# 290 TensorE products in 25 forms placed behind the last stage of a float32 transformer kernel

## What is computed

```python
for i in range(4):                       # first block
    x = x + 0.5 * rms_norm(swiglu_ffn(rms_norm(x, g[0]), w_gate_up[i, 0], w_down[i, 0]), g[1])
    y = mixer_a / mixer_b / mixer_c / mixer_a (rms_norm(x, g[2]), memory of 256 rows, ...)
    x = x + rms_norm(y, g[3])
    x = x + 0.5 * rms_norm(swiglu_ffn(rms_norm(x, g[4]), w_gate_up[i, 1], w_down[i, 1]), g[5])
for i in range(4):                       # second block: nsa, stick breaking, conv, moba
    x = x + mixer_i(_rms_norm(x, attn_norm[i]), ...)
    hm = _rms_norm(x, mlp_norm[i])
    x = x + jnp.square(jax.nn.relu(hm @ mlp_w_up[i])) @ mlp_w_down[i]
return x
```

## Time and profile before

| what | value |
|---|---|
| median of 2 runs | 3338.68 us (3338.37 to 3338.98) |
| span of the profiled execution, first to last instruction | 3335.1 us |
| TensorE matmuls busy | 3215.7 us, 96% of the span, 19661 instructions |
| VectorE busy | 1953.3 us, 59% |
| ScalarE busy | 1628.6 us, 49% |
| mean granted TensorE clock | 0.992 |

### The profile page before, as it was taken

One profiled execution on the slowest core, in us unless ns is written; L12 is line 12 of the kernel. 1 busy time (PEld: TensorE's weight loads), 2 busy tenths in 40 slices (PEclk: granted clock), 3 DMA queues, 4 the chain that ended last, 5 costly groups with the idle time before them and its releaser, 6 DMA issues.

```text
span 3335.1 us, 52167 instructions
## 1 busy us (share of the span) xinstructions
PE 3215.7 (96%) x19661; PEld 2816.0 (84%) x19661; DVE 1953.3 (59%) x2911; ACT 1628.6 (49%) x2426; POOL 135.6 (4%) x230
## 2 busy tenths in 40 slices
PE   7999999999999999999999999999999999999999
PEld 7977988977898977897987897779788888987797
DVE  4566556665555554655656656565566558656663
ACT  5445444445444435544545545554354446545552
POOL 1000000000000000000000101000000000001000
PEclk9999999999999999999999999999999999999999
DMA  6654656652555543565654554435444551555354
GB/s 215 194 174 133 201 177 192 189 157 89 175 185 185 180 157 114 158 190 166 206 192 152 179 190 152 140 112 184 162 158 142 187 179 33 195 189 164 116 200 152
DMA packets 413280, 551.71 MB, mean 165 GB/s; under 512 B 33952, under 2 KB 263520, under 8 KB 413104
## 3 DMA queue, kind: packets, MB, share of 16 engines
q1 hardware_dynamic: 409248, 536.10, 50.1%
q0 software_dynamic: 2864, 10.38, 1.0%
q10 hardware_dynamic: 992, 2.84, 0.2%
HBM read 548.15 MB, written 1.05 MB: 165 GB/s over the span
## 4 chain that ended last, share of the span: by engine, by line
PE 87%; DVE 8%; ACT 3%; issue 1%; POOL 0%; DMA 0%; SPq 0%; DVEq 0%; ACTq 0%
PE G L796 16%; PE G L800 15%; PE G L797 15%; PE G L897 11%; PE G L899 11%; PE G L898 11%; DVE ring_lo_sb L1977 3%; PE T L775 2%; PE S L1000 1%; PE O L1028 1%; DVE act_hi_sb L1991 1%; ACT ring_hi_sb L1438 1%; DVE act_lo_sb L2001 1%; DVE work_sb L2181 0%; PE G L1307 0%
## 5 line engine op out<-in xcount | busy, mean ns | idle before, releaser
L1977 DVE TENSOR_TENSOR ring_lo_sb<-ring_sb,ring_hi_sb 128x1024 fp32r<-128x1024 f32 (+1 forms) x1028 | 1222.4, 1209 | 620.2 <-ACT ring_hi_sb L1438 602.4
L1438 ACT ACTIVATE ring_hi_sb<-ring_sb 128x1024 fp32r<-128x1024 f32 (+1 forms) x1028 | 1056.7, 1044 | 693.3 <-DMA ring_sb<-ffn_w_down 218.3
L897 PE MATMUL G<-act_hi_sb,ring_hi_sb 128*128 128x256 f32 x3136 | 876.4, 279 | 3.0 <-DVE ring_lo_sb L1977 3.0
L898 PE MATMUL G<-act_lo_sb,ring_hi_sb 128*128 128x256 f32 x3136 | 872.3, 278 | 0.0
L899 PE MATMUL G<-act_hi_sb,ring_lo_sb 128*128 128x256 f32 x3136 | 872.3, 278 | 0.0
L897 PEld LDWEIGHTS G<-act_hi_sb,ring_hi_sb 128*128 128x128 f32 x3136 | 589.5, 188 | 3.3 <-issue 3.2
L796 PE MATMUL G<-ring_hi_sb,hid_hi_sb 128*128 128x512 f32 x1456 | 581.0, 399 | 10.3 <-DVE hid_hi_sb L2010 6.5
L899 PEld LDWEIGHTS G<-act_hi_sb,ring_lo_sb 128*128 128x128 f32 x3136 | 589.8, 188 | 0.0
L898 PEld LDWEIGHTS G<-act_lo_sb,ring_hi_sb 128*128 128x128 f32 x3136 | 588.3, 188 | 0.0
L797 PE MATMUL G<-ring_lo_sb,hid_hi_sb 128*128 128x512 f32 x1456 | 576.9, 396 | 0.0
L800 PE MATMUL G<-ring_hi_sb,hid_lo_sb 128*128 128x512 f32 x1248 | 492.5, 395 | 0.0
(11 more groups left out here) (274 smaller groups left out, 2543.1 us busy)
## 6 DMA issues: line engine op xcount, KB each, us to landing
ring_sb<-ffn_w_gate_up SPq DMA_DIRECT2D x704, 256.0 KB, 4.0
ring_sb<-ffn_w_down SPq DMA_DIRECT2D x352, 256.0 KB, 3.8
ring_sb<-mlp_w_up SPq DMA_DIRECT2D x256, 256.0 KB, 3.8
ring_sb<-mlp_w_down SPq DMA_DIRECT2D x256, 256.0 KB, 3.7
ring_sb<-a_w_in SPq DMA_DIRECT2D x48, 256.0 KB, 4.4
ring_sb<-sb_w_in SPq DMA_DIRECT2D x48, 256.0 KB, 4.0
ring_sb<-moba_w_in SPq DMA_DIRECT2D x48, 256.0 KB, 4.0
ring_sb<-w_mem_kv SPq DMA_DIRECT2D x32, 256.0 KB, 3.8
```

What stands on the lines that cost most here:

```text
L897: mm(dst, hi, act_hi[:, kt, :], start=(kt == 0 and f == 0), stop=False, skip_group_check=True)
L898: mm(dst, hi, act_lo[:, kt, :], start=False, stop=False, skip_group_check=True)
L1438: fn(ring_hi[:, s_, :, 0:w], ring[:, s_, :, 0:w], ACT.Copy).then_inc(hi_ready, 1)
L1977: v.tensor_tensor(ring_lo[:, s_, :, 0:w], ring[:, s_, :, 0:w], ring_hi[:, s_, :, 0:w], ALU.subtract).then_inc(lo_ready, 1)
```

## The change

At the end of TensorE's stream, behind the loop over the stages, code is added that issues 25 blocks. A block is 8, 11 or 12 rounded products into the PSUM bank `T[0]` (in one block `T[0]` and `T[1]` in turn) and then one float32 transpose of the constant `from_on` into the same bank, which marks the block's end in a trace. No product waits for a semaphore or raises one, and nothing reads what they write. No other engine's code changes.

```diff
                 elif kind == "conv":
                     conv()
+            def flat(b, at):
+                return b[:, at, :, :].rearrange("p k n -> p (k n)")
+
+            def block_of(n_mm, lhs, rhs, bank=lambda j: 0, first=lambda j: j == 0):
+                for j in range(n_mm):
+                    w, m = lhs(j), rhs(j)
+                    b = T[bank(j)]
+                    dst = b[0:w.shape[1], 0:int(np.prod(m.shape[1:]))]
+                    if len(m.shape) == 3:
+                        dst = dst.rearrange("p (a n) -> p a n", a=m.shape[1])
+                    mm(dst, w, m, start=first(j), stop=True, skip_group_check=True)
+                nc.tensor.transpose(T[0][:, 0:P], from_on, ident)
+
+            def tail_forms():
+                a_flat = act_hi[:, :, :].rearrange("p k n -> p (k n)")
+                h_flat = hid_hi[:, :, :].rearrange("p k n -> p (k n)")
+
+                def acts(off=0, m=P, step=1):
+                    return lambda j: a_flat[:, 2 * P * (j % 6) + off:2 * P * (j % 6) + off + m * step:step]
+
+                def units(off=0, n=HALF, step=1):
+                    return lambda j: flat(ring_hi, j % RING)[:, off:off + n * step:step]
+                block_of(12, acts(), units())
+                block_of(12, acts(m=32), units())
+                block_of(12, acts(), units(off=8))
+                block_of(12, acts(), units(off=16))
+                block_of(12, acts(), units(off=32))
+                block_of(12, acts(off=16), units())
+                block_of(12, acts(off=8), units())
+                block_of(12, acts(step=2), units())
+                block_of(12, acts(), units(step=2))
+                block_of(12, acts(), lambda j: ring_hi[:, j % RING, :, 0:SEQ])
+                block_of(12, acts(), units(n=480))
+                block_of(12, acts(), units(n=448))
+                block_of(12, acts(), units(n=384))
+                block_of(12, acts(), units(n=320))
+                block_of(12, acts(), units(), bank=lambda j: j % 2)
+                block_of(12, acts(), units(), first=lambda j: True)
+                block_of(12, lambda j: flat(ring_hi, j % RING)[:, 0:P], lambda j: h_flat[:, HALF * j:HALF * (j + 1)])
+                block_of(12, lambda j: a_flat[:, 0:P], lambda j: flat(ring_hi, 0)[:, 0:HALF])
+                block_of(8, lambda j: a_flat[:, 0:P], lambda j: flat(ring_hi, 0)[:, 0:64])
+                for n in (264, 272, 282, 300, 320, 340):
+                    block_of(11, acts(), lambda j, n=n: flat(ring_hi, j % RING)[:, 0:n if j == 0 else SEQ])
+            tail_forms()
```

## The result

The changed kernel took 3394.35 us (median of 3387.9 and 3400.8) against 3338.68 us before, a ratio of 1.0169 with an interval of 1.0143 to 1.0195. Forecast were 3397.0 us and +1.7%, within a range of 3390 to 3403. The two executions of the changed kernel lie 12.9 us apart, those of the kernel before 0.6 us. That spread turned out to be the part of the case that I had not foreseen, and most of the experiments are about it.

What follows compares the result with a forecast made beforehand. TensorE, with matmuls busy 96% of the span, was taken as the bound; 62.5 us of added work from 3330.60, behind 4.5 us of cover, lengthens the span 58.3 us, giving 3397.0 us (+1.7%), range 3390 to 3403.

Steps and rivals of the forecast that it cites:

- What bounds the end: End of the span: TensorE done at 3330.60, then idle 4.5 us until the store lands, covering that much added work.
- the sign of being wrong: End of the span: more than 0.5 us after TensorE's last transpose would show the prediction wrong.
- The price by columns: Added products: cost goes by columns, 0.4557 ns each, 0.2333 us for 512; thirteen ordinary blocks 36.4 us.
- the rival of a lost fast path: Added blocks: one shifted or stepped form priced as plain float32, 7.5 us above the ordinary price; chance 0.13.
- The cover of the stepped stationary operand: Block with every second element stationary: a weight load of twice 106 ns stays hidden, ordinary price of 0.2333 us a product.
- The stepped moving operand: Block whose moving operand takes every second element: twice the ordinary price, 5.6 us, between bounds of 2.8 and 10.3 us.
- Narrow products: Block of eight 64-column products: about 0.12 us each, 1.0 us together, limited by the 128-column weight load.
- The array's rate: Rival for the 168 wide products: all at 0.2133 us, 3.4 us less, and the step free, 2.8 us less; chance 0.09.
- The clock: Added work: granted clock stays 1.0; the half clock would add 0.19 us a wide product, sharing chance 0.10 with several slow forms.
- The other price for 512 columns: Wide added products: the skill's columns/2.4 GHz + 2.5 ns gives 216 ns, making the sum about 4 us smaller.
- The 3.6 us that I put outside the span: Measured time beyond the profiled span: 3.6 us, taken to stay, so the median of 3338.7 becomes 3397.0.
- The sign that I named for the added code reaching back: VectorE's last addition and the store: should start at 3330.80 and 3332.05 as now; if they move, added code reaches back.

Runs made afterwards that it cites:

- the single block: Changed kernel with only the first of its 25 blocks kept; the span ended 4.7 us after mlp's last product started, as without the block.
- the doubled work: Changed kernel with all 25 blocks issued twice, against the kernel before: 3456.7 us against 3336.8 us, ratio 1.035.
- the five rounds: Changed kernel again, nothing edited, beside the kernel before: 3400.4 us against 3341.4 us, ratio 1.0175.
- a lead of another width than 256: Kernel before plus one unread product of such a width ahead of each of the 12 loops; with 264 columns 3355.7 us against 3337.4 us.

## Why the prediction held, point by point

*What bounds the end.* Right. TensorE's last old product, the addition and the store kept their distances, the cover was the 4.5 us read from the earlier trace rows, TensorE's last transpose ended 0.24 us before the span did (the sign of being wrong was 0.5), and both the single block (nothing to pay) and the doubled work (62 us more) bear it out.

*The price by columns.* Right. From L1420 to L1420 with the transpose: the thirteen ordinary blocks of 512 columns took 2.83 to 2.92 us, forecast 2.91; 480, 448, 384 and 320 columns 2.72, 2.54, 2.24 and 1.88, forecast 2.74, 2.56, 2.21 and 1.86; the last blocks about 1.4, forecast 1.4. No shift and no stepped stationary operand showed, so the rival of a lost fast path fell for all of them. The cover of the stepped stationary operand is real: a load with a step of 4, which sets 235 ns beside 256 moving columns, leaves 238 beside 512. But the load with a step of 2 is not twice as slow as I allowed for (2 x 106 = 212 ns): beside 256 moving columns the distance is 121 ns, so the load takes at most that. A transpose's 0.11 us stands in two places: the next product starts 0.03 us behind it, and the one after that is 0.32 us away instead of 0.23.

*The stepped moving operand.* 5.55 us with its transpose against 5.7 forecast. The size was right and the grounds were not. I took it to be twice the price because half of every fetched piece would be wasted; then either pairs on an even element (pieces of two elements) should be cheaper than a step of 2, or a step of 4 (pieces of four) dearer. Steps of 2, 3 and 4 and all three sorts of pairs cost 227 to 233 ns. So twice the price was a choice between two bounds that came out well, not a mechanism understood. Why one or two neighbours in a run halve the rate stays open.

*Narrow products.* 0.98 us for the block with its transpose against 1.07; the distance is 112 ns and comes from the load of 128 stationary columns: with 32 of them 64 columns cost 32 ns.

*The array's rate.* That some form would run at the 0.2133 us of the array was given 0.09, and none did. Rounded products of 512 columns with 32 stationary ones, in two banks, without accumulation or with the same operands all stood at 0.23.

*The clock.* 1.00 through the tail, and through twice the tail. In the trace after, the last stretch at 0.5 ends at 2521 us.

*The other price for 512 columns.* The 216 ns that the prediction takes from the Trainium skill (TensorE: Matmul & The Clock Gate, section "Back-to-back issue gap") stand on that page for a single product by itself. For a stream, which is what the tail is, the page gives about 131 ns, and the 233 ns of the rounded products here lie above both.

*The step that was missing* is in the use of the two medians. The 3.6 us that I put outside the span were the difference between a median and another execution's span; where the profiled execution has its own time (3387.9 and 3386.2), it is 1.7 us. And I took two runs within 0.6 us for the kernel's spread. It is 20 us, most of it from which pace the loops take. The sign that I named for the added code reaching back, an addition that no longer starts at 3330.80, came true (3323.94) without its reaching back; an absolute time was the wrong thing to watch, and the distance of 0.43 us from the last product the right one. The forecast of 58.3 us stood up against 58.0 in the trace, but single executions lie anywhere between 41 and 75 us apart, by the extremes of the five rounds (3388.7 less 3347.6 and 3402.3 less 3327.3): the first pair of medians gave 55.7, the next 59.0. That the median of two executions fell into a range 13 us wide was in part luck: 3387.9 lay below it and 3400.8 inside, and of the seven executions of the changed kernel two lay below.

## What to carry to other kernels

Work put behind the last thing that anybody waits for costs the sum of the distances between starts, less the cover up to the last store's landing; read that distance from the timeline's starts, by columns, and not from durations. When two traces of nearly the same kernel differ somewhere that the change doesn't touch, lay the starts of one engine side by side before believing a mechanism. And where a product's time has two values, count products in equal windows of both traces, since a mean over the kernel hides it.

## What the runs showed of the hardware

Long streams of rounded products with 256 moving columns run at 113 or at 118 ns at the same granted clock, and keep the pace that they have at the entry for the 768 products of an ffn's loop and across the semaphore waits of a loop. Over eight profiles of kernels with the loops as before, 42 of 96 loops were fast. Which one a loop takes was changed at will in one direction only (a lead of another width than 256: 48 of 48 slow; of 256 columns: 14 of 24 fast). What picks it, and what the array is waiting for in the slow one, was not found.

A dense rounded product pays 233 ns for 512 columns where the array's clock would allow 213; shifts, banks, accumulation and the number of stationary columns don't change it. A moving operand with one or two neighbours in a run pays double (227 to 233 ns for 256 columns), with four or more it doesn't (113 to 121 ns); three were not tried. The load of 128 stationary columns takes about 110 ns of its own: products of 64, 128 and 192 columns are 112 ns apart, and with 32 stationary columns those of 64 and 128 are 32 and 60 ns apart.
